# Two FFN blocks in float32: down products opened by bank halves, an up product's first unit by tile

## The reference

```python
mod = silu(c) @ w_ada + b_ada                 # shift, scale, gate: 6 x 2048 numbers
x = x + gate_m * (mix @ w_out)
h = rms_norm(x) * (1 + scale_f) + shift_f
u = causal_dwconv(h @ w_up, 3 taps)           # 2048 -> 2 x 5632
x = x + gate_f * ((silu(g) * val) @ w_down)   # g, val = halves of u;  5632 -> 2048
```

## Time and profile before

| | |
|---|---|
| median of 3 runs | 2658.02 us (2657.28 to 2660.94) |
| the profiled execution | 2658.35 us, span 2656.6 us |
| PE busy | 2455.1 us, 92% of the span |
| DVE busy | 1886.6 us, 71% |
| ACT busy | 1113.7 us, 42% |
| mean granted TensorE clock | 0.96 of full |
| HBM read | 607.54 MB, 230 GB/s over the span |

### The profile page before, as it was taken

How to read it: one execution, slowest core, us unless ns; L and a number is a source line. 1 busy time by engine, 2 the same in 40 slices (tenths; PEclk the granted TensorE clock), 3 DMA queues, 4 the chain that set the end, 5 groups by cost and what they waited for, 6 DMA issues and landing times.

```text
span 2656.6 us, 51242 instructions
## 1 busy us (share of the span) xinstructions
PE 2455.1 (92%) x21552; PEld 2378.8 (90%) x21552; DVE 1886.6 (71%) x2243; ACT 1113.7 (42%) x1179; POOL 95.9 (4%) x184
## 2 busy tenths in 40 slices
PE   4899976999999999999989998999999999999997
PEld 4899746989999999999979887889999999999997
DVE  6988878877877767876788666667877544555545
ACT  3244323355544324443453445434555433344433
POOL 0020000000000000000000000000000000000000
PEclk8999958999999999999999999899999999999999
DMA  8988815957677877777759322217576445455452
GB/s 359 420 323 328 323 69 198 367 195 277 257 297 263 336 287 269 271 271 310 271 186 355 119 103 94 93 56 263 210 281 243 184 160 188 174 178 186 180 200 95
DMA packets 87919, 613.63 MB, mean 231 GB/s; under 512 B 9576, under 2 KB 13168, under 8 KB 14320
## 3 DMA queue, kind: packets, MB, share of 16 engines
q1 hardware_dynamic: 64608, 442.95, 44.6%
q0 software_dynamic: 23184, 168.83, 16.7%
HBM read 607.54 MB, written 4.21 MB: 230 GB/s over the span
## 4 chain that ended last, share of the span: by engine, by line
PE 77%; DVE 13%; DMA 4%; ACT 4%; issue 2%; SPq 0%; DVEq 0%; POOLq 0%; ACTq 0%
PE ps L721 23%; PE ps L722 22%; PE ps L723 22%; DMA ada_raw<-in_ada_stream 2%; DVE first_raw L1560 2%; DVE w_lo L1548 2%; DMA w_raw<-in_w_stream 1%; DVE ada_raw L1560 1%; DMA first_raw<-in_ada_stream 1%; PE ps L718 1%; ACT w_hi L1071 1%; PE ps L607 1%; PE ps L501 1%; DVE tmp L1587 1%; PE ps L751 1%
## 5 line engine op out<-in xcount | busy, mean ns | idle before, releaser
L721 PE MATMUL ps<-h_hi,w_hi 128*128 128x256 f32 x4480 | 1284.8, 287 | 81.3 <-DVE h_lo L1673 34.2
L722 PE MATMUL ps<-h_lo,w_hi 128*128 128x256 f32 x4480 | 1275.6, 285 | 0.0
L723 PE MATMUL ps<-h_hi,w_lo 128*128 128x256 f32 x4480 | 1275.2, 285 | 0.0
L721 PEld LDWEIGHTS ps<-h_hi,w_hi 128*128 128x128 f32 x4480 | 868.1, 194 | 91.7 <-DVE h_lo L1673 36.3
L1544 DVE TENSOR_TENSOR w_lo<-w_raw,w_hi 128x2048 fp32r<-128x2048 f32 x299 | 683.0, 2287 | 310.3 <-ACT w_hi L1065 310.1
L722 PEld LDWEIGHTS ps<-h_lo,w_hi 128*128 128x128 f32 x4480 | 868.5, 194 | 0.4
L723 PEld LDWEIGHTS ps<-h_hi,w_lo 128*128 128x128 f32 x4480 | 868.0, 194 | 0.0
L1065 ACT CAST w_hi<-w_raw 128x2048 fp32r<-128x2048 f32 x298 | 567.2, 1907 | 688.0 <-DMA w_raw<-in_w_stream 680.0
L721 PE MATMUL ps<-hid_hi,w_hi 128*128 (+1 forms) x1344 | 380.5, 283 | 28.1 <-issue 21.8
L1560 DVE SCALAR_TENSOR_TENSOR ada_raw<-ada_raw,ada_c 128x2048 f32<-128x2048 f32 x160 | 365.3, 2285 | 44.4 <-DMA ada_raw<-in_ada_stream 44.1
L723 PE MATMUL ps<-hid_hi,w_lo 128*128 (+1 forms) x1344 | 380.0, 283 | 0.0
(11 more groups left out here) (355 smaller groups left out, 1615.5 us busy)
## 6 DMA issues: line engine op xcount, KB each, us to landing
w_raw<-in_w_stream SPq DMA_DIRECT2D x372, 1024.0 KB, 4.9
ada_raw<-in_ada_stream POOLq DMA_DIRECT2D x160, 1024.0 KB, 7.2
first_raw<-in_ada_stream SPq DMA_DIRECT2D x32, 1024.0 KB, 10.1
kept_raw<-in_w_stream SPq DMA_DIRECT2D x4, 1024.0 KB, 7.2
x<-in_x_t SPq DMA_DIRECT2D x1, 2048.0 KB, 9.7
x_kept<-x SPq DMA_DIRECT2D x1, 2048.0 KB, 13.4
out_t<-x SPq DMA_DIRECT2D x4, 512.0 KB, 2.8
ada_c<-in_c SPq DMA_DIRECT2D x1, 1024.0 KB, 4.7
```

The source lines that it names most:

```text
L721: mm(o, hi, r_hi, start=first, stop=False, **kw)
L722: mm(o, hi, r_lo, start=False, stop=False, **kw)
L723: return mm(o, lo, r_hi, start=False, stop=last, **kw)
```

## The change

Five edits, which belong together:

1. **PE, start of each down product.** The first two units go over the 8 tiles of the first four banks (`down_order`), then over the other 8. The first half waits only for the evacuation of the chunk before last, the second half for that of the last chunk. `units_used` is incremented in the second half.
2. **ACT and DVE, last chunk of each up product.** `hi` and `lo` of the down product's unit 1 are moved ahead of the evacuation of the last chunk (`ahead`). The output product keeps the old order (`False`).
3. **PE, first chunk after 1A and 2A.** Its first unit runs one output tile after the other (12 matmuls each), and each waits only for its own bank; `down_evac` is incremented after each two tiles.
4. **DVE, end of 1A and 2A.** `lo` of the next unit 1 is moved ahead of the 16 additions to x.
5. **DVE, modulation.** Products 154 to 156 leave the last group of 1B. All later ones up to 169 move by three places, and three are done in the output product of the second block, after the additions of its units 5, 6 and 7.

```diff
@@ PE: chunk
-            def chunk(u0, e0, n0, kind, n_all=UNITS, i0=0):
+            def chunk(u0, e0, n0, kind, n_all=UNITS, i0=0, added=None):
...
+                        elif kind == "cols" and added is not None and i == 0:
+                            for j in range(4):
+                                pe.wait_ge(down_evac, added + j + 1)
+                                for k in range(4):
+                                    w = slice(k * 512 + j * P, k * 512 + j * P + P)
+                                    last = three(bank(4 * par_ + j), w_h[:, w], w_l[:, w], h_hi[:, k], h_lo[:, k],
+                                                 k == 0, False)
@@ PE: down
-                pe.wait_ge(act_evac, e_next + 2)
-                pe.wait_ge(dve_evac, e_next + 2)
-
                 def body(b, first=False):
-                    for i in range(4):
+                    for i in range(2 if first else 0, 4):
...
+                order = down_order(e_next)
+                pe.wait_ge(hid_lo_s, hc0 + 1)
+                for half in range(2):
+                    pe.wait_ge(act_evac, e_next + 1 + half)
+                    pe.wait_ge(dve_evac, e_next + 1 + half)
+                    for i in range(2):
+                        pe.wait_ge(lo_ready, u0 + i + 1)
+                        w_h, w_l = w_hi[:, slot_of(i, u0)], w_lo[:, slot_of(i, u0)]
+                        for j in order[8 * half:8 * half + 8]:
+                            w = slice(j * P, j * P + P)
+                            last = three(ps[:, j // 2, (j % 2) * T:(j % 2) * T + T], w_h[:, w], w_l[:, w], hid_hi[:, i],
+                                         hid_lo[:, i], i == 0 and j % 2 == 0, False, skip_group_check=True)
+                        if half:
+                            last.then_inc(units_used, 1)
                 body(0, True)
@@ PE: after 1A (after 2A the same with added=8 and 16)
             down(U_DN1A, 0, UP1B, 2 * FFN_A)
-            pe.wait_ge(down_evac, 2)
-            chunk_runs(pe, 0, 1, UP1B, chunk(U_UP1B, UP1B, N_F1, "cols"))
-            pe.wait_ge(down_evac, 4)
+            chunk(U_UP1B, UP1B, N_F1, "cols", added=0)(0, UP1B % 2)
+            pe.wait_ge(down_evac, 8)
@@ ACT: stream (finish on DVE alike, with lo)
                 hi(0, 0, u_next)
+                if ahead:
+                    hi(0, 1, u_next)
                 for f in evac:
                     f(c1 - 1, (e0 + c1 - 1) % 2)
-                hi(0, 1, u_next)
+                if not ahead:
+                    hi(0, 1, u_next)
@@ DVE: down
                 if name is not None:
-                    body(n // 4 - 1, 0, True)
+                    lo_kept(name, 0)
+                    lo_unit(u0 + n - 4)
+                    lo_kept(name, 1)
+                    lo_unit(u0 + n - 3)
                     return
                 lo(0, 0, u_next)
+                lo(0, 1, u_next)
...
-                    if k % 4 == 3:
+                    if k % 2:
                         last.then_inc(down_evac, 1)
-                lo(0, 1, u_next)
@@ DVE: second block
-            pair = 157
+            pair = 154
...
             for j in (5, 6, 7):
                 lo_unit(U_OUT2 + (7, 8, 9)[j - 5])
                 add_half(j)
+                one_ada(WKV_ADA - 3 + j - 5)
```

More of the change, by code:

```diff
@@ L771, in body @@
                             last = three(o, w_h[:, w], w_l[:, w], at(hid_hi, 4 * b + i),
-                                         at(hid_lo, 4 * b + i), first and i == 0 and j % 2 == 0, False,
-                                         skip_group_check=True)
+                                         at(hid_lo, 4 * b + i), False, False, skip_group_check=True)
                         last.then_inc(units_used, 1)
+                order = down_order(e_next)
[12 more added lines that the diff above has]
+                            last.then_inc(units_used, 1)
                 body(0, True)
@@ L957, in _ @@
             down(U_DN2A, FFN_A + FFN_B, UP2B, 2 * FFN_A)
-            pe.wait_ge(down_evac, 6)
-            chunk_runs(pe, 0, 1, UP2B, chunk(U_UP2B, UP2B, N_F2, "cols"))
-            pe.wait_ge(down_evac, 8)
+            chunk(U_UP2B, UP2B, N_F2, "cols", added=8)(0, UP2B % 2)
+            pe.wait_ge(down_evac, 16)
             chunk_runs(pe, 1, FFN_B, UP2B, chunk(U_UP2B, UP2B, N_F2, "cols"))
@@ L1091, in norm, with stream @@
                     A(h_hi[:, dst + k], tmp[:, (n0 + k) % 4], ACT.Identity, bias=shifts[k]).then_inc(n_hi, 1)
-            def stream(u0, e0, c0, c1, evac, u_next):
+            def stream(u0, e0, c0, c1, evac, u_next, ahead=True):
                 hi(c0, 2, u0)
@@ L1244, in down @@
                     hi(0, 1, u_next)
-            stream(U_OUT1, OUT1, 0, 4, skip_evac(U_OUT1), U_UP1A)
+            stream(U_OUT1, OUT1, 0, 4, skip_evac(U_OUT1), U_UP1A, False)
             act.wait_ge(dve_evac, UP1A + 2)
@@ L1269, in _ @@
             hi(0, 0, U_DN1A)
+            hi(0, 1, U_DN1A)
             for f in ev:
                 f(11, (UP1A + 11) % 2)
-            hi(0, 1, U_DN1A)
             down(U_DN1A, 2 * FFN_A, U_UP1B)
@@ L1598, in gains_of, with finish, stream @@
                 return [gain[:, k:k + 1] for k in range(KT)]
-            def finish(c, e0, evac, u_next):
+            def finish(c, e0, evac, u_next, ahead=True):
                 lo(0, 0, u_next)
+                if ahead:
+                    lo(0, 1, u_next)
                 for f in evac:
                     f(c, (e0 + c) % 2)
-                lo(0, 1, u_next)
-            def stream(u0, e0, c0, c1, evac, p0, pairs, u_next=None):
+                if not ahead:
+                    lo(0, 1, u_next)
+            def stream(u0, e0, c0, c1, evac, p0, pairs, u_next=None, ahead=True):
                 def some_ada(c, i, odd):
@@ L1632, in stream @@
                 if u_next is not None:
-                    finish(c1 - 1, e0, evac, u_next)
+                    finish(c1 - 1, e0, evac, u_next, ahead)
             def plain_body(u0, evac):
@@ L1904, in down, with some_ada, body @@
             def down(u0, n, gate0, p0, pairs, e_next, done, u_next=None, name=None):
-                def body(b, first, kept=False):
+                def some_ada(b, i):
+                    for q in ada_after(pairs, i):
+                        ada(pairs * b + (p0 + q), (pairs * b + p0 + q) % 2)
+                def body(b):
                     for i in range(4):
-                        if kept and i % 2 == 0:
-                            lo_kept(name, i // 2)
-                        elif kept:
-                            lo_unit(u0 + n - 4 + i // 2)
-                        elif i >= first:
-                            lo(b, i, u0)
-                        for q in ada_after(pairs, i):
-                            ada(pairs * b + (p0 + q), (p0 + q) % 2 if pairs == 2 else (pairs * b + p0 + q) % 2)
-                body(0, 2)
+                        lo(b, i, u0)
+                        some_ada(b, i)
+                lo(0, 2, u0)
+                some_ada(0, 1)
+                lo(0, 3, u0)
+                some_ada(0, 2)
+                some_ada(0, 3)
                 if pairs == 3:
                     for b in range(1, n // 4 - (name is not None)):
-                        body(b, 0)
+                        body(b)
                 else:
                     with dve.Fori(1, n // 4 - (name is not None)) as b:
-                        body(b, 0)
+                        body(b)
                 if name is not None:
-                    body(n // 4 - 1, 0, True)
+                    lo_kept(name, 0)
+                    lo_unit(u0 + n - 4)
+                    lo_kept(name, 1)
+                    lo_unit(u0 + n - 3)
                     return
                 lo(0, 0, u_next)
+                lo(0, 1, u_next)
                 mod_bias(gate0, KT)
@@ L1962, in _ @@
             finish(11, UP1A, ev, U_DN1A)
-            down(U_DN1A, 2 * FFN_A, GATE_F, 104, 3, UP1B, 4, U_UP1B)
+            down(U_DN1A, 2 * FFN_A, GATE_F, 104, 3, UP1B, 8, U_UP1B)
             stream(U_UP1B, UP1B, 0, FFN_B, hidden(UP1B, FFN_A, "fcw"), 122, 2, U_DN1B)
@@ L2096, in _ @@
             finish(11, UP2A, ev, U_DN2A)
-            down(U_DN2A, 2 * FFN_A, MODS + GATE_F, 0, 0, UP2B, 8, U_UP2B)
+            down(U_DN2A, 2 * FFN_A, MODS + GATE_F, 0, 0, UP2B, 16, U_UP2B)
             stream(U_UP2B, UP2B, 0, FFN_B, hidden(UP2B, 2 * FFN_A + FFN_B, "fcw2"), 0, 0, U_DN2B)
```

3 lines of the change are left out of this document (1 added, 2 removed).

## The result

| | before | after |
|---|---|---|
| median | 2657.65 us (2656.61 to 2660.94, 4 runs) | 2626.42 us (2622.34 to 2633.75, 4 runs) |
| ratio | | 0.9883, 95% interval 0.986 to 0.9907 |
| the profiled execution | 2658.35 us, span 2656.6 | 2626.51 us, span 2624.8 |

What follows compares the result with a forecast made beforehand. PE, 77% of the span in the chain that ended last, was taken as the bound; 29.5 - 4.5 + 6.9 + 7.9 = 39.8 us off the profiled 2658.35 gave 2618.5 us (median 2618), range 2609 to 2634.

Steps and rivals of the forecast that it cites:

- The starts: Four down product starts: 21.8 us of waits and 8.9 of clock go, less 1.2 left over: 29.5 us.
- Unit 4 in 1A and 1B: PE newly waits for unit 4, 1.7 us in 1A and 2.8 in 1B, clock kept: 4.5 us lost.
- The end of 1B: Wait for the last `w_lo` falls from 6.4 to 2.5 us and 3.0 of clock is kept: 6.9 us gained.
- After 1A and 2A: Two waits for additions to x fall from 3.4 to 1.0 us; with 3.1 of clock, 7.9 us gained.
- The moved products: Three products moved into the second output product fit in DVE's time there: cost 0, at worst 2 us.
- The slower rival: Second output product: DVE falls behind PE, units 5 to 15 each open a gap; 2674 us, chance 0.03.
- The clock's price: Low-clock stretches on PE: each microsecond counted as half lost, such as 10 x 0.20 = 2.0 us before 1A.
- DMA holds 1A and 1B: Rival: weights can't follow an earlier PE, so the shifts in 1A and 1B are lost; 2628 us, chance 0.16.
- the forecast's sign of 10: Forecast wrong if 1A and 1B weight loads land over 10 us after issue, making PE wait at units 5 to 12.
- The clock falls at what is left: Rival: the two longer remaining waits, 2.8 and 2.5 us in 1B, lose the clock; 2624 us, chance 0.13.
- The moved `hi` holds up the evacuation: Rival: late unit 1 load delays ACT's taps at one or two starts; 2624 to 2630 us, chance 0.06.
- the halves don't overlap as written: Rival at down product starts: something else ended the 5.4 us waits; included in the late `hi` rival's chance, 0.06.

Runs made afterwards that it cites:

- the ladder: Changed kernel with nine rising waits put into PE's list in the second block's last up product; gaps of 0.39 to 3.68 us, no total time given.
- the other three traces: Changed kernel profiled again (2627.32 us), changed kernel with `lo` of unit 1 put back behind the additions (2631.23 us), and the ladder (no time given).
- the second profile of after: The changed kernel run again without any edit, beside other runs; 2627.32 us, ratio 0.9877.
- edits 3 and 4 alone: The kernel before with only edits 3 and 4 of the change; 2650.8 us, ratio 0.9975.

## Why the prediction came out as it did

The terms outside 1B came about as forecast. In 1B two waits stayed long enough to lose the clock, which is the second rival; the range held since it had that case in it.

- **The starts** (29.5 us of waits and clock): right. Every wait of 5.4 us went, all four windows read 1.00, and a `w_lo` wait of 0.3 to 0.4 us is left (0.3 taken). S4, which is nearly the start of 2A alone, gained 8.0 and 7.3 us against 7.1.
- **Unit 4 in 1A and 1B** (4.5 us without clock): the mechanism was right, a size and the clock were off. In 1A the product's load took 4.9 us (5.5 taken) and the wait was 0.7, not 1.7. In 1B it took 6.4 (5.3 in before) and the wait was 3.9, not 2.8, with 1.7 us of clock lost behind it. The forecast called 2.8 "nearer to the 2.1 us that kept it"; by the ladder 2.8 would have lost it as well. This is the part that failed every time: in the other three traces with the same lists in 1B the wait was 4.1, 3.9 and 4.4 us, and the clock fell behind each.
- **The end of 1B** (6.9 us): the step that failed most in the profiled execution. The wait of 2.5 was taken from DVE's list. It was 3.3, since unit 17's load took 10.0 us, where before had 7.0, and DVE sat idle 1.19 us for it; and the 3.0 us of clock, counted as won, stayed lost. Even the forecast 2.5 would have lost the clock (the ladder's 2.40 did). S2 got 8.5 us of its 16.0; 1.1 of wait and 1.5 of clock at unit 4, and 0.8 and 3.0 here, make 6.4 of the missing 7.5. But this load varies: in the other three traces the end waited 1.4, 1.6 and 0 us, less than forecast, and kept the clock. In the second profile of after S2 got 11.0.
- **After 1A and 2A** (7.9 us): right in the waits (1.1 against 1.0) and the clock; 6.9 us by the run of edits 3 and 4 alone, 2.0 of them in S3. What it left out is a late `lo` 1, which in the second profile of after held up the additions and cost 1.1 us and the clock.
- **The moved products** (0): right. DVE's rows for units 5 to 7 of the output product:

```profile
1783.05 0.87 DVE L2054 SCALAR_TENSOR_TENSOR x<-ps,mod,x 128x256 f32<-128x256 f32 x2
1783.83 2.28 DVE L1579 SCALAR_TENSOR_TENSOR ada_raw<-ada_raw,ada_c 128x2048 f32<-128x2048 f32 x1
...
1788.25 0.87 DVE L2054 SCALAR_TENSOR_TENSOR x<-ps,mod,x 128x256 f32<-128x256 f32 x2
...
1793.45 0.87 DVE L2054 SCALAR_TENSOR_TENSOR x<-ps,mod,x 128x256 f32<-128x256 f32 x2
```

  The earlier trace rows show the additions of units 5 and 7 (not "7 to 9"). Unit 5's are now 14.2 us earlier, those of unit 7 only 10.8, so DVE was up to 3.4 us late. But PE has no new wait there, and the last additions are 14.2 us earlier again. The slower rival (2674) had no part.
- **The clock's price.** A low microsecond was counted as half lost. In before, matmuls at 1.2 GHz start every 0.213 us, and at 2.4 GHz every 5.60/48 = 0.117 us. So it passes 0.55 of the work and costs 0.45: 13.5 us and not 15.0 for all clock terms. The Trainium skill, "TensorE: Matmul & The Clock Gate", section "Wait — 56ns, not 53.3ns?", gives N/1.2 ns between the starts of back-to-back matmuls at the low clock and N/2.4 + 2.5 at the high; for 256 columns that is 213 ns, as measured, and 109, where this stream of weight loads and matmuls has 117.
- **DMA holds 1A and 1B** (rival, 2628): its number is near the median, but it isn't the cause. With one product moved, S2 fell by 6 to 9 us at the same weight traffic. What is true of it is local: one load beside others took 10 us. One of a kept unit took even 10.9, over the forecast's sign of 10, but PE didn't wait for it. The 5 us from 1220 in the trace after read 433 GB/s, and the 65.6 us of the second slice on its page 421. The Trainium skill, "DMA: Bandwidth & Descriptors", section "Where 436 GB/s comes from", has about 358 GB/s as the bound from HBM to SBUF; this case doesn't bear it out.
- **The clock falls at what is left** (rival, 2624): this is what happened, in both places of 1B. The forecast's own sign of being wrong, "if the clock falls after gaps under 3 us", came as well, though not in the first profile: the clock fell behind 2.23 us in the second profile of after and behind 2.40 and 2.83 in the ladder. One trace, with one gap that kept the clock and none between it and 3.4 us, could not show where it turns.
- **The moved `hi` holds up the evacuation** and **the halves don't overlap as written** (rivals): neither came. No start of either profile of after has a wait over 0.4 us between the halves.

What stays open: in S5 PE's idle time and low clock fell by 7.3 + 0.9 x 5.1 = 11.9 us (the clock's loss at 0.45 in place of 0.5), and the stage by 9.8 and 10.5. Some 0.9 us of the first is the unit time (below); 1.2 and 1.4 us aren't explained.

## What to carry to other kernels

A wait that is halved isn't half paid: price each residue against the gap that loses the clock in this very trace, and build a ladder of gaps where the decision falls between two rows, with more than one gap of each length near the turn. When a consumer is moved off a busy stretch, look at who prefetches for it; here the loads stayed behind, beside the one weight load that PE was waiting for. One profile of a load that varies isn't its size: the wait at unit 4 stood in all four traces with its order, the one at the end was anything from 0 to 3.3 us. And compare by stage, since another stage's clock can hide or fake a gain of 5 us.
